# Output projections of a two-layer backbone: one float32 product against three float32r products of split operands

## The reference

```python
yl = jnp.concatenate([att_l, conv_l], axis=-1) @ w_out        # first layer, latent; the same for the context
yl = (jax.nn.gelu(gl) * (hs_l[0] + hs_l[1])) @ w_out          # second layer, latent alone
xl = xl + m_l[2] * yl
hl = modulate(rmsnorm(xl, norm_ffn_g[l]), m_l[3], m_l[4])
aff = jax.nn.softmax((h @ router_w).astype(jnp.float32), axis=-1)
```

## Time and profile before

| | us |
|---|---|
| median of 3 runs | 3438.24 (3436.93 to 3440.89) |
| profiled execution | 3435.6 |
| its span, first to last instruction | 3433.7 |
| stage o0, first DMA issue to the last transpose | 598.88 to 789.76 |
| stage o1, first DMA issue to the last of the affinities | 2350.04 to 2512.17 |

### The profile page before, as it was taken

How to read it: one execution, slowest core, us unless ns; L and a number is a source line. 1 busy time by engine, 2 the same in 40 slices (tenths; PEclk the granted TensorE clock), 3 DMA queues, 4 the chain that set the end, 5 groups by cost and what they waited for, 6 DMA issues and landing times. The chain is left out here.

```text
span 3433.7 us, 59934 instructions
## 1 busy us (share of the span) xinstructions
PE 3010.1 (88%) x24830; PEld 2463.3 (72%) x24830; DVE 2087.6 (61%) x2181; ACT 1779.9 (52%) x1984; POOL 569.2 (17%) x266
## 2 busy tenths in 40 slices
PE   6599877996799999999999969997929999999993
PEld 2488744452688888888888856774529999999993
DVE  0422376235566666666666645973357888888884
ACT  2411145232555555555555546883337777777773
POOL 1011043001011111111111124651030000000000
PEclk8699889997899999999999989998959999999996
DMA  7211100227688778777778730103248999999995
GB/s 326 79 38 37 56 1 4 96 86 307 234 275 270 261 264 271 271 268 263 274 274 273 261 131 22 44 27 110 87 165 313 348 387 357 352 377 367 354 348 177
DMA packets 137950, 726.08 MB, mean 211 GB/s; under 512 B 10708, under 2 KB 13524, under 8 KB 109828
## 3 DMA queue, kind: packets, MB, share of 16 engines
q1 hardware_dynamic: 125064, 684.99, 53.1%
q0 software_dynamic: 12288, 37.75, 4.6%
q10 hardware_dynamic: 384, 0.24, 0.0%
HBM read 680.90 MB, written 42.04 MB: 211 GB/s over the span
## 5 line engine op out<-in xcount | busy, mean ns | idle before, releaser
L1653 DVE TENSOR_TENSOR mixed_low<-mixed_raw,mixed_high 128x3072 fp32r<-128x3072 f32 (+1 forms) x192 | 593.1, 3092 | 349.2 <-ACT mixed_high L1587 347.6
L1587 ACT CAST mixed_high<-mixed_raw 128x3072 fp32r<-128x3072 f32 (+1 forms) x192 | 490.0, 2554 | 482.9 <-DMA mixed_raw<-in_moe 482.7
L2074 DVE TENSOR_TENSOR rows_low<-rows_raw,rows_high 128x2816 fp32r<-128x2816 f32 x188 | 581.4, 3093 | 80.3 <-ACT rows_high L2018 71.0
L2018 ACT CAST rows_high<-rows_raw 128x2816 fp32r<-128x2816 f32 x188 | 479.3, 2558 | 111.9 <-PE ps L1925 67.2
L1509 PE MATMUL ps<-mixed_high,mixed_xhi 128*128 128x384 f32 (+1 forms) x1024 | 343.3, 335 | 0.5 <-DVE mixed_low L1653 0.5
L1923 PE MATMUL ps<-rows_high,rows_xhi 128*128 128x352 f32 x1024 | 337.4, 329 | 6.0 <-issue 4.5
L1925 PE MATMUL ps<-rows_high,rows_xlo 128*128 128x352 f32 x1024 | 330.1, 322 | 0.0
L1924 PE MATMUL ps<-rows_low,rows_xhi 128*128 128x352 f32 x1024 | 329.7, 322 | 0.0
L1511 PE MATMUL ps<-mixed_high,mixed_xlo 128*128 128x384 f32 (+1 forms) x1024 | 329.7, 322 | 0.0
L1510 PE MATMUL ps<-mixed_low,mixed_xhi 128*128 128x384 f32 (+1 forms) x1024 | 329.6, 322 | 0.0
L1497 PE MATMUL ps<-mixed_raw,mixed_xc 128*32 128x96 f32 (+1 forms) x8192 | 186.9, 243 | 42.1 <-ACT mask_sb L1609 27.0
(11 more groups left out here) (293 smaller groups left out, 5949.5 us busy)
## 6 DMA issues: line engine op xcount, KB each, us to landing
rows_raw<-in_moe_rows SPq DMA_DIRECT2D x192, 1408.0 KB, 7.8
mixed_raw<-in_moe SPq DMA_DIRECT2D x144, 1536.0 KB, 6.4
ring_r<-in_ada_w SPq DMA_DIRECT2D x24, 2048.0 KB, 17.5
mixed_raw<-in_moe SPq DMA_DIRECT2D x48, 1024.0 KB, 6.4
w_raw_r<-in_ev_in SPq DMA_DIRECT2D x18, 512.0 KB, 3.3
w_raw_u<-in_od_in SPq DMA_DIRECT2D x16, 512.0 KB, 3.3
x_res<-ring_r SPq DMA_DIRECT2D x10, 512.0 KB, 2.6
x_norm<-ring_r SPq DMA_DIRECT2D x10, 512.0 KB, 2.8
```

The costliest lines, as they stand in the source:

```text
L1587: act.copy(r.high[:, p % SLOTS, 0:nj, :], r.raw[:, p % SLOTS, 0:nj, :]).then_inc(high_done, 1)
L1653: dve.tensor_tensor(r.low[:, p % SLOTS, 0:nj, :], r.raw[:, p % SLOTS, 0:nj, :], r.high[:, p % SLOTS, 0:nj, :].bitcast(F32), ALU.subtract). ...
L2018: act.copy(high[:, p % SLOTS, :], raw[:, p % SLOTS, :]).then_inc(high_done, 1)
L2074: dve.tensor_tensor(low[:, p % SLOTS, :], raw[:, p % SLOTS, :], high[:, p % SLOTS, :].bitcast(F32), ALU.subtract).then_inc(low_done, 1)
```

## The change

In both output projection stages the float32 matmuls are replaced. The weights arrive in eight pieces of 512 KB (slice k, all 1024 columns) in a ring of three raw buffers. ScalarE casts piece k to float32r (`w_high`), VectorE subtracts the cast from the raw piece (`w_low`), and SP loads piece k+3 into the raw buffer once that is done. All eight loads stand ahead of the gate rows, of the router weights (now last of the three) and of the token tiles in SP's queue. Token tiles are split two ahead: ScalarE casts 8 slices of 128x128 (`token_high`), GpSimd subtracts (`in_low`). TensorE makes six products per slice k (two halves of the outputs, three products each); for tile 0 it waits for each slice's low part in turn, so that the first tile's products follow the pieces. The wait for gates and router moves from the stage's start to before the second group of transposes. The weights of o0 are no longer loaded during attention. To make room, the output stages have buffers of their own (`OutBuffers`), and region B or C, whichever the stage does not read, is not allocated while one runs; the choice stage after o0 has its scratch regions allocated anew.

```diff
--- before.py
+++ after.py
@@ -841,14 +852,7 @@
         piece_at = {x: i for i, x in enumerate(pieces)}
         last_piece = [max(piece_at[x] for x in pieces if x[0] == n) for n in range(NT)]
 
-        out_w_in = semaphore(nc, ctx, "at_wout")
         block = ctx.enter_context(nc.Block())
-
-        @block.sync
-        def _(sp):
-
-            sp.dma_start(m.ring[:, 10 * D:18 * D].rearrange("p (k n) -> p k n", k=K), d["ev_out"]).then_inc(out_w_in, 16)
-            sp.wait_ge(out_w_in, 16)
 
         @block.tensor
         def _(pe):
@@ -1042,29 +1046,41 @@
 
 
 
+class OutBuffers:
+
+
+    def __init__(self, nc, ctx, where):
+        sb = lambda name, shape, dt=F32: ctx.enter_context(nc.sbuf_tensor(f"{name}_{where}", shape, dt))
+        self.raw = sb("raw", [P, OUT_RAW, D])
+        self.w_hi, self.w_lo = (sb(x, [P, K, D], F32R) for x in ("whi", "wlo"))
+        self.in_hi, self.in_lo = (sb(x, [P, 2, K, P], F32R) for x in ("inhi", "inlo"))
+        self.xt, self.x1, self.xn, self.gates = (sb(x, [P, 2, D]) for x in ("xt", "x1", "xn", "gates"))
+        self.junk = sb("junk", [P, D])
+        self.h2 = sb("h2", [P, 2, K, P])
+        self.rw = sb("rw", [P, K, NE])
+        self.st = sb("st", [P, 2, 8])
+        self.lg = sb("lg", [P, 2, 2, NE])
+
+
+OUT_RAW = 3
+
+
 def out_stage(nc, m, d, name, layer, inT, w_dram, sources, affT):
     tiles = []
     for src, n, s in sources:
         tiles += [(src[i * P:(i + 1) * P, :], s) for i in range(n)]
     N = len(tiles)
-    w = m.ring[:, 10 * D:18 * D].rearrange("p (k n) -> p k n", k=K)
-    at = 0
-    xt = m.ring[:, at:at + 2 * D].rearrange("p (b n) -> p b n", b=2)
-    x1 = m.ring[:, at + 2 * D:at + 4 * D].rearrange("p (b n) -> p b n", b=2)
-    xn = m.ring[:, at + 4 * D:at + 6 * D].rearrange("p (b n) -> p b n", b=2)
-    gates = m.ring[:, at + 6 * D:at + 8 * D].rearrange("p (b n) -> p b n", b=2)
-    junk = m.ring[:, at + 8 * D:at + 9 * D]
-    h2 = m.A[:, 0:2 * D].rearrange("p (b k t) -> p b k t", b=2, k=K)
-    rw = m.A[:, 2 * D:2 * D + K * NE].rearrange("p (k e) -> p k e", k=K)
-    st = m.A[:, 2 * D + 256:2 * D + 512].rearrange("p (b x) -> p b x", b=2)
-    lg = m.A[:, 2 * D + 512:2 * D + 512 + 4 * NE].rearrange("p (b x e) -> p b x e", b=2, x=2)
+    o = m.out
+    xt, x1, xn, gates, h2, st, lg = o.xt, o.x1, o.xn, o.gates, o.h2, o.st, o.lg
+    junk, rw = o.junk[:, :], o.rw[:, :, :]
     with stage_of(nc) as ctx:
         aux_in, y_done, y_read, sq, chain, sd_done, xn_done, turned, ev_act, ev_dve = semaphores(
             nc, ctx, " ".join(f"{name}_{x}" for x in
                               "aux y yread sq chain sd xn turn eva evd".split()))
         lg_done, nmax, ex_done, aff_done, afft_done, afft_out, x1_done, aff_clear = semaphores(
             nc, ctx, " ".join(f"{name}_{x}" for x in "lg nmax ex aff afft afftout x1 affclear".split()))
-        w_in = [semaphore(nc, ctx, f"{name}_w{half}") for half in range(2)]
+        w_in = [semaphore(nc, ctx, f"{name}_w{b}") for b in range(OUT_RAW)]
+        w_high, w_low, in_high, in_low = semaphores(nc, ctx, " ".join(f"{name}_{x}" for x in "whi wlo ihi ilo".split()))
         x_in, x1_out, xn_out = ([semaphore(nc, ctx, f"{name}_{x}{b}") for b in range(2)]
                                 for x in ("xin", "x1o", "xno"))
         block = ctx.enter_context(nc.Block())
@@ -1078,14 +1094,14 @@
 
         @block.sync
         def _(sp):
-            sp.dma_start(rw, d["router_w"][layer]).then_inc(aux_in, 16)
+            for k in range(K):
+                if k >= OUT_RAW:
+                    sp.wait_ge(w_low, k - OUT_RAW + 1)
+                sp.dma_start(o.raw[:, k % OUT_RAW, :], w_dram[:, k, :]).then_inc(w_in[k % OUT_RAW], 16)
             for s in range(2):
                 row = d["mrow"][s:s + 1, (layer * 6 + 2) * D:(layer * 6 + 3) * D]
                 sp.dma_start(gates[:, s, :], row.to_broadcast((P, D))).then_inc(aux_in, 16)
-            if w_dram is not None:
-                for half in range(2):
-                    at = slice(half * BANK, (half + 1) * BANK)
-                    sp.dma_start(w[:, :, at], w_dram[:, :, at]).then_inc(w_in[half], 16)
+            sp.dma_start(rw, d["router_w"][layer]).then_inc(aux_in, 16)
             for t, (src, s) in enumerate(tiles):
                 if t >= 2:
                     sp.wait_ge(x1_done, t - 1)
@@ -1101,12 +1117,16 @@
         def _(pe):
             def project(t):
                 pe.wait_ge(y_read, t - 1) if t >= 2 else None
-                for half in range(2):
-                    if t == 0 and w_dram is not None:
-                        pe.wait_ge(w_in[half], 16)
-                    for k in range(K):
-                        mm = pe.matmul(m.ps[:, 2 * (t % 2) + half, :], inT[:, k, t * P:(t + 1) * P],
-                                       w[:, k, half * BANK:(half + 1) * BANK], start=(k == 0), stop=(k == K - 1))
+                pe.wait_ge(in_low, t + 1)
+                b = t % 2
+                for k in range(K):
+                    if t == 0:
+                        pe.wait_ge(w_low, k + 1)
+                    for half in range(2):
+                        out, at = m.ps[:, 2 * b + half, :], slice(half * BANK, (half + 1) * BANK)
+                        pe.matmul(out, o.in_hi[:, b, k, :], o.w_hi[:, k, at], start=(k == 0), stop=False)
+                        pe.matmul(out, o.in_hi[:, b, k, :], o.w_lo[:, k, at], start=False, stop=False)
+                        mm = pe.matmul(out, o.in_lo[:, b, k, :], o.w_hi[:, k, at], start=False, stop=(k == K - 1))
                 mm.then_inc(y_done, 1)
 
             def turn(t):
@@ -1134,10 +1154,11 @@
                     pe.wait_ge(afft_out, t)
                 pe.transpose(m.ps[0:NE, 7, 0:P], lg[:, t % 2, 1, :], m.ident[:, :]).then_inc(afft_done, 1)
 
-            pe.wait_ge(aux_in, 48)
             for t in range(N + 3):
                 if t < N:
                     project(t)
+                if t == 2:
+                    pe.wait_ge(aux_in, 48)
                 if 1 <= t <= N:
                     turn(t - 1)
                 if 2 <= t <= N + 1:
@@ -1147,7 +1168,21 @@
 
         @block.scalar
         def _(act):
+            def token_high(t):
+                if t >= 2:
+                    act.wait_ge(y_done, t - 1)
+                act.copy(o.in_hi[:, t % 2, :, :], inT[:, :, t * P:(t + 1) * P]).then_inc(in_high, 1)
+
+            token_high(0)
+            for k in range(K):
+                b = k % OUT_RAW
+                act.wait_ge(w_in[b], 16 * (k // OUT_RAW + 1))
+                act.copy(o.w_hi[:, k, :], o.raw[:, b, :]).then_inc(w_high, 1)
+                if k == 1:
+                    token_high(1)
             for t in range(N + 2):
+                if t + 2 < N:
+                    token_high(t + 2)
                 if t < N:
                     b, s = t % 2, tiles[t][1]
                     act.wait_ge(x1_done, t + 1)
@@ -1172,6 +1207,13 @@
                         act.wait_ge(aff_clear, 1)
                     act.copy(affT(t - 2), m.ps[0:NE, 7, 0:P]).then_inc(afft_out, 1)
 
+        @block.gpsimd
+        def _(pool):
+            for t in range(N):
+                pool.wait_ge(in_high, t + 1)
+                pool.tensor_tensor(o.in_lo[:, t % 2, :, :], inT[:, :, t * P:(t + 1) * P],
+                                   o.in_hi[:, t % 2, :, :].bitcast(F32), ALU.subtract).then_inc(in_low, 1)
+
         @block.vector
         def _(dve):
             steps = semaphores(nc, ctx, f"{name}_links")[0]
@@ -1185,6 +1227,10 @@
 
 
             dve.memset(choice_rows(m), -2.0).then_inc(aff_clear, 1)
+            for k in range(K):
+                dve.wait_ge(w_high, k + 1)
+                dve.tensor_tensor(o.w_lo[:, k, :], o.raw[:, k % OUT_RAW, :], o.w_hi[:, k, :].bitcast(F32),
+                                  ALU.subtract).then_inc(w_low, 1)
             dve.wait_ge(aux_in, 48)
             for t in range(N + 1):
                 if t < N:
@@ -2543,14 +2589,18 @@
             (m.split, lambda: norm_stage(nc, m, "n0", 0, [(d["x"], 0, LT, 0), (d["ctx"], 0, NT - LT, 1)])),
             (m.split, lambda: even_in_stage(nc, m, d)),
             (m.plain, lambda: attention_stage(nc, m, d)),
-            (m.plain, lambda: out_stage(nc, m, d, "o0", 0, chunked(m.B), None,
+        ]
+        first_out = [
+            (m.for_out, lambda: out_stage(nc, m, d, "o0", 0, chunked(m.B), d["ev_out"],
                                         [(d["x"], LT, 0), (d["ctx"], NT - LT, 1)], affT)),
+        ]
+        first_choice = [
             (m.plain, lambda: choose_stage(nc, m, "c0", True, lambda nc, ctx: AdaUnits(nc, ctx, m, d, 1, 4))),
         ]
         mixed_stages = [(m.for_mixed, lambda: expert_mixed_stage(nc, m, d, "e0", 0))]
-        second_stages = [
-            (m.split, lambda: odd_mixer_stage(nc, m, d)),
-            (m.plain, lambda: out_stage(nc, m, d, "o1", 1, chunked(m.C), d["od_out"],
+        second_stages = [(m.split, lambda: odd_mixer_stage(nc, m, d))]
+        second_out = [
```

(1 more changed line is left out.)

## The result

| | before | after |
|---|---|---|
| median of the runs, us | 3439.56 (3436.93 to 3445.97, 4 runs) | 3397.32 (3397.05 to 3399.04, 4 runs) |
| profiled execution, us | 3435.6 | 3397.05 |
| its span, us | 3433.7 | 3395.3 |
| stage o0, first DMA issue to the next stage's, us | 192.0 | 165.0 |
| stage o1, the same, us | 163.0 | 138.5 |

The ratio is 0.9873, 95% interval 0.9859 to 0.9888: faster and clear of noise, as forecast, but by 44 us and not by 57, and 3397.3 lies 3.3 us above the range of 3371 to 3394.

The account below looks back on a forecast made before the run. TensorE was taken to bound the output stages' steady part. 45.4 us from steady tiles plus 12.0 from first tiles made 57.4, so 3435.6 became 3378.2, or 3380.8 as the median of runs; range 3371 to 3394 us.

Parts of the forecast that it names:

- the steady period: Tiles after the first in o0 and o1: TensorE's period becomes 13.59 us, 2.84 us less per tile, 45.4 us together.
- the work beside it: Token cast and GpSimd subtraction per tile: cast hidden, VectorE's second sum blocked and 2.15 us later, cost counted as 0.
- The slack: Steady tiles: VectorE's loop of 13.0 us against TensorE's 13.59, so TensorE still ends last by 0.5 us.
- The rival that VectorE's loop becomes the bound: Steady tiles: slower GpSimd subtraction makes VectorE's loop set the period, costing 4 us, up to 24 us; chance 0.12.
- the order of issue: Start of each output stage: gates queued behind the weight pieces arrive at 22.0 us, hidden with 2.3 us to spare.
- the first tile, the term of 12.0 us: First tile of o0 and o1: products end 21.0 us after the first issue, gaining 4.1 and 7.9 us.
- piece 5, issued at 11.4, lands at 14.7: First tile's weight loads, us from the stage's first issue: 3.3 us from issue to landing; this piece split at 17.05.
- landing 4.5 us each: First tile: slower weight pieces cost 2 us in each of three rounds, 6 per stage, 3392.8; chance 0.17 with slow clock.
- The last test that the prediction named: Output stages: prediction is wrong if the second tile's first products start later than 24 us after the first issue (S).
- the clock: First tile: TensorE begins at the lower clock and reaches the higher one some 5 us into its products.
- The rival of a slow first tile: First tile at the lower clock throughout: ends at S+26.9 in both stages, 11.8 us lost, 3392.6; chance 0.17 with slow pieces.
- the basis: Whole kernel: gain subtracted from the profiled 3435.6 us, giving 3378.2; the median of runs taken as 2.6 above it.

Follow-up runs that it names:

- e10_float32: Changed kernel with one float32 product of the high parts in place of three float32r products, all loads, casts and subtractions kept: 3433.94 us.
- e9_no_token_low: Changed kernel with all three products, but GpSimd's token subtraction nearly all left out from the third tile on: 3389.72 us.
- e7_one_product: Changed kernel with only the high x high product, the two products with a low part left out: 3375.97 us.
- e8_one_no_low: Changed kernel with only the high x high product and nearly all of GpSimd's token subtraction left out from the third tile on: 3350.30 us.
- e6_gates_first: Changed kernel with gate rows and router weights issued ahead of the weight pieces, three raw buffers: 3394.91 us.
- e2_after_again: The changed kernel run once more with no edit: 3393.74 us, ratio 0.9862 to the kernel before.
- e5_six_raw: Changed kernel with six raw buffers in place of three: 3378.95 us, ratio 0.9825 to the kernel before.
- e11_four_raw: Changed kernel with four raw buffers in place of three: 3395.50 us in one execution.
- e4_only_o1: The change in output stage o1 only, o0 left as in the kernel before: 3418.81 us, ratio 0.9933.

## Why the prediction was right or wrong

**Right: the steady period.** 13.59 us forecast, 13.59 measured, 0.227 us a product, in both stages; 45.3 of the 45.4 us. e10_float32 shows that the products alone give it.

**Right: the work beside it.** The second sum was to take about 3.4 us and took 3.21 here, 2.95 in most periods; the 1.08 us from the end of GpSimd's instruction to the end of VectorE's, read in the recurrent block, is here 718.81 + 3.21 less 718.55 + 2.39, 1.08 again, and 1.08 or 1.09 for each of the 14 tiles of both stages that have it. The slack was 0.5 to 0.8 us in the steady periods with the block; e9_no_token_low shows that the block costs no time beside three products, e7_one_product and e8_one_no_low that it costs 1.7 us where VectorE's loop is the bound. The rival that VectorE's loop becomes the bound fell: GpSimd took 2.39 us and not 3.25.

**Right: the order of issue.** e6_gates_first is the worse one. The DMA issues of this stretch of the kernel after (KB each, median us from issue to landing):

```profile
gates_o<-mrow SPq DMA_DIRECT2D x2, 512.0 KB, 5.5
xt_o<-in_x SPq DMA_DIRECT2D x2, 512.0 KB, 7.5
```

Issued at S+15.6, the gates were there at about S+21 to 22, as forecast, though after 5.5 us and not 7.7; the token tiles behind them came later, and VectorE's first tile was released by one of these, at S+24.3 instead of 22.0. That did not reach TensorE. Its first transposes start at S+34.1, right behind the second tile's products (23.2 + 10.9 = 34.1).

**Wrong: the first tile, the term of 12.0 us**, which measured 6.2 (and 0.6 in e2_after_again, by the same working). The step that failed is "piece 5, issued at 11.4, lands at 14.7": a landing of 3.3 us, the median of another stage, was put as a constant into a ring whose issue hangs on it. Pieces 2 and 3 were split at S+11.0 and 12.1 (11.3 and 12.6 forecast), but 4 at 15.2 instead of 13.9 and 7 at 21.7 instead of 19.6. Piece 4 was issued after piece 1's subtraction, at 606.7, and cast at 611.86: 5.2 us. The median of the earlier trace rows is over 18 loads, of which all but the first few go alone, with the engines at 36 GB/s (us 150 to 180 in the kernel before); its first two, issued 0.5 us apart, took 3.9 and 4.7 us, and the cast at 138.20 in the earlier trace rows could have told it. The rival named for this, "landing 4.5 us each", had the size of the landing exactly, 4.5 and 4.6 us median; it was priced at 6 us a stage, and the stages lost 2.6 and 3.2 (5.7 each in e2_after_again). The last test that the prediction named, second tile at S+24 or later, was passed in the first trace (S+23.2 and 23.9) and failed in the second (S+25.1 and 25.5). Chance 0.17 together with the slow clock was too little for it, since no row showed 3.3 us under these conditions. e5_six_raw and e11_four_raw close the proof: the first tiles end earlier the fewer loads depend on a subtraction, and with six buffers they give 14 us. That the time is then 3378.95, near the 3380.8 of the prediction, is luck: it is another kernel, whose loads took 7.2 us.

The DMA page of the Trainium skill ("DMA: Bandwidth & Descriptors", Anatomy of one DMA) fits one DMA of the path that GpSimd issues, not of the queue used here, as 2.0 us and its bytes at 436 GB/s: 3.2 us for 512 KB, an estimate, which agrees with the 3.3 of the earlier trace rows and not with the 4.5 measured here. The same section of the Trainium skill says that completion makes up most of the fixed part; a ring would pay it in each round, which fits the low stretches in the row of GB/s above, but no run here separates it.

**In between: the clock.** In the kernel after it rose after 2.7 us of products in o0 and 4.8 in o1, sooner than the 5 us assumed, and in o0 this hid some of the slow landing. In e2_after_again it fell again after a wait of 2.2 us. The rival of a slow first tile (the lower clock throughout, because of the bursts) came true for about 1.6 us of its 5.9, and of the two traces only in this one.

**Wrong: the basis.** The sum was made against the profiled 3435.6 us, whose stages outside o0 and o1, 3078.8 us, are the shortest of all these traces; the kernel after met 3091.8. That is 13.0 of the 18.9 us by which its profiled execution missed 3378.2; the first tiles are the other 5.8. The three runs of the kernel before, 3436.93 to 3440.89, gave no hint that it goes from 3430.93 to 3450.81 within seven runs on one chip, and up to 3452.75 on another. By ratio, which is free of that, the gain was 44 (after) and 47 us (e2_after_again) against 57, 12 us short on the mean of the two; the output stages of the two traces were 5.9 and 11.5 us short, 9 on the mean, so most of it lies there, and the 3 us left are within the intervals of about 5 us. Why the experts' stage takes 1152 us in one execution and 1166 in another is open; the change doesn't do it, since the kernel before took 1160 once and e6_gates_first 1154. The range held the milder of the two misses, and not both.

## What to carry to other kernels

A latency is worth what it is under the load and the dependence it will have: where the issue of load k+n waits for the use of load k, price a whole round (landing, cast, subtraction), take the landing from a loaded stretch, and ask first for the depth at which the queue never runs dry, since three more buffers of 4 KB a partition shortened the two stages here by 8 us (13 against the second trace). When a pass of a product gets 3.8 times cheaper (0.859 to 0.227 us), look at the loop of the other engines: half a microsecond of slack was enough, and it could be read from one period of the trace before. Where a kernel has a long stage whose length differs between executions, forecast the difference or the ratio, and put that scatter, not that of three runs, into the range of the absolute time.

## What was not expected of the hardware

- Loads of 512 KB with up to two others in flight landed in 3.5 to 5.6 us (median 4.5, o0 of the kernel after), with up to five others in 3.7 to 9.4 (median 7.2, o0 of e5_six_raw), though the engines moved some 260 GB/s in the first case (us 602 to 621) and some 380 in the second (602 to 616). A load issued alone in the input projection of the kernel before took 3.1 to 3.9 us. What makes a load take 5.2 us with one or two others in flight wasn't settled.
- A VectorE sum of two SBUF operands that met a GpSimd subtraction ended 1.08 or 1.09 us after it, in each of the 14 tiles in the kernel after, whether it had started 0.01 or 1.5 us behind GpSimd.
- The granted clock fell 1 us after a 2.2 us wait in the middle of products (e2_after_again), though TensorE had been busy at the higher level before it, and waits of about 1 us in the kernel after did not do that.
- Where TensorE waits 3 us in every period (e7_one_product) the granted clock is 0.62 to 0.71 over a period, and VectorE's loop, which has TensorE's transposes and router products in it, goes from 12.7 to 13.1 us up to 14.35 whenever the transposes fall into the lower level: less work on TensorE made its part of another engine's loop slower.
- The first experts' stage, with the same instructions, took 1152 (before) to 1166 us (e4_only_o1) at a granted clock of 0.98, and TensorE's idle time in it went from 73 to 84 us.
